# Modulation vectors computed with the conditioning vectors as 32-column weights, four chunks of the sum in four quarters of the TensorE array

## The reference, cut to what matters

```python
mod_ctx = (jax.nn.silu(c_ctx) @ w_mod[l] + b_mod[l])[None, None, :]
mod_lat = (jax.nn.silu(c) @ w_mod[l] + b_mod[l])[:, None, :]
...
sh1, sc1, g1, sh2, sc2, g2 = jnp.split(mod.astype(x.dtype), 6, axis=-1)
h = rmsnorm(x, norm1_g) * (1 + sc1) + sh1
m, st = mixer(h, w_in, ...)        # projections, RG-LRU scans, pooling, w_up_rnn, w_o
x = x + g1 * m
h = rmsnorm(x, norm2_g) * (1 + sc2) + sh2
x = x + g2 * peer(h, ...)          # 8 heads, top-16 product keys, expert rows
```

## Time and profile before

| | |
|---|---|
| median of 3 runs | 2282.52 us (2277.72 to 2285.01) |
| profiled execution, its own time | 2282.51 us |
| its span in the trace | 2280.2 us |
| PE busy | 2170.3 us, 95% of the span |
| DVE busy | 1673.6 us, 73% |
| ACT busy | 799.4 us, 35% |
| POOL busy | 775.4 us, 34% |
| mean granted TensorE clock | 0.964 of full |

### The profile page before, as it was taken

How to read it: one execution, slowest core, us unless ns; L and a number is a source line. 1 busy time by engine, 2 the same in 40 slices (tenths; PEclk the granted TensorE clock), 3 DMA queues, 4 the chain that set the end, 5 groups by cost and what they waited for, 6 DMA issues and landing times.

```text
span 2280.2 us, 34404 instructions
## 1 busy us (share of the span) xinstructions
PE 2170.3 (95%) x11688; PEld 1941.6 (85%) x11688; DVE 1673.6 (73%) x3317; ACT 799.4 (35%) x1028; POOL 775.4 (34%) x519
## 2 busy tenths in 40 slices
PE   5889998899999999999599999999999999999998
PEld 2789998899999888888488889998888888888887
DVE  4448998142449679999878888886777777777784
ACT  1435554211332322222144455554222222222222
POOL 1122331322123388888442222210222322322240
PEclk8999999899799999999799999999999999999997
DMA  8212213233422388888477777764999889989991
GB/s 354 84 52 65 66 61 115 98 121 130 163 78 66 114 265 283 292 290 285 151 281 290 292 269 289 283 254 161 309 320 310 305 312 363 310 308 310 318 325 66
DMA packets 167478, 502.06 MB, mean 220 GB/s; under 512 B 16608, under 2 KB 74336, under 8 KB 165600
## 3 DMA queue, kind: packets, MB, share of 16 engines
q1 hardware_dynamic: 101872, 273.96, 35.0%
q0 software_dynamic: 46080, 167.79, 21.4%
q10 hardware_dynamic: 19440, 59.25, 6.5%
HBM read 436.45 MB, written 64.50 MB: 220 GB/s over the span
## 4 chain that ended last, share of the span: by engine, by line
PE 75%; DVE 16%; DMA 2%; issue 2%; POOL 2%; ACT 2%; SPq 0%; ACTq 0%; DVEq 0%; POOLq 0%
PE P L787 29%; PE P L533 20%; PE P L702 14%; PE P L724 4%; PE P L551 3%; DVE rowsX L1430 2%; DVE rows L1430 2%; PE P L619 1%; POOL wLo L467 1%; DVE oh L1468 1%; DMA tb<-in_posT 1%; DVE oh L1461 1%; DVE keysel L1472 1%; PE P L755 1%; PE P L667 1%
## 5 line engine op out<-in xcount | busy, mean ns | idle before, releaser
L811 ACT ACTIVATE wHi<-raw 128x1024 fp32r<-128x1024 f32 x330 | 346.3, 1049 | 1257.3 <-PE P L787 459.2
L702 PE MATMUL P<-hHi,wHi 128*128 128x480 f32 x1024 | 397.1, 388 | 30.0 <-POOL wLo L467 29.8
L702 PE MATMUL P<-hHi,wLo 128*128 128x480 f32 x1024 | 390.6, 381 | 0.0
L702 PE MATMUL P<-hLo,wHi 128*128 128x480 f32 x1024 | 390.1, 381 | 0.0
L461 POOL TENSOR_TENSOR wLo<-raw,wHi 128x1024 fp32r<-128x1024 f32 (+1 forms) x76 | 186.6, 2457 | 511.3 <-ACT wHi L811 511.2
L1538 DVE TENSOR_TENSOR wLo<-raw,wHi 128x1024 fp32r<-128x1024 f32 x188 | 230.3, 1225 | 172.2 <-ACT wHi L811 171.3
L483 POOL DMA_INDIRECT rows<-in_v_tab,Eg x160 | 175.2, 1095 | 531.5 <-DVE htok L1589 248.8
L533 PE MATMUL P<-hHi,wHi 128*128 128x320 f32 x960 | 230.3, 321 | 23.4 <-POOL wLo L461 10.6
L702 PEld LDWEIGHTS P<-hHi,wHi 128*128 128x128 f32 x1024 | 193.9, 189 | 63.6 <-issue 33.0
L533 PE MATMUL P<-hLo,wHi 128*128 128x320 f32 x960 | 222.3, 313 | 0.0
L533 PE MATMUL P<-hHi,wLo 128*128 128x320 f32 x960 | 221.9, 312 | 0.0
(11 more groups left out here) (231 smaller groups left out, 3878.0 us busy)
## 6 DMA issues: line engine op xcount, KB each, us to landing
raw<-in_ublk SPq DMA_DIRECT2D x128, 512.0 KB, 4.5
raw<-in_v_tab SPq DMA_DIRECT2D x128, 512.0 KB, 5.7
raw<-in_wblk SPq DMA_DIRECT2D x104, 512.0 KB, 3.7
gel_scratch<-gel ACTq DMA_DIRECT2D x128, 240.0 KB, 4.2
gsr<-gel_scratch SPq DMA_DIRECT2D x128, 240.0 KB, 5.9
gate_scratch<-stage ACTq DMA_DIRECT2D x6, 4096.0 KB, 14.9
gates4a<-gate_scratch SPq DMA_DIRECT2D x16, 768.0 KB, 7.4
gates4b<-gate_scratch SPq DMA_DIRECT2D x16, 768.0 KB, 7.6
```

Source lines behind the costliest of these rows:

```text
L702: last = nc.tensor.matmul(P[0][:, j % 2, 0:TD], w_[:, j % 2, k * 128:(k + 1) * 128], x_[:, k, C0:T], start=(k == 0 and a == 0 and b == 0), ...
L811: return nc.scalar.activation(out, in_, f, **kw)
```

## The change

Modulations 16 to 39 are computed another way; 40 to 47 stay. DVE writes the conditioning vectors into `c32`, eight chunks of 32 columns, of which 2 hold the vectors and 30 are zero. `modulation_parts` (L568 of the changed file) takes a chunk of `c32` as weights and lets the 128 columns of the block's chunk pass through. Chunks 0 to 3 go to the four column quarters of the array and so to the partitions 0, 32, 64 and 96 on of `P[2]`; chunks 4 to 7 are added to them there. ACT copies the 128 x 128 result to `mrow` (`mod_rows`), and `modulation_turn` (L577) uses it as weights against two columns of `same`, which sums the four quarters and turns the result into the two columns of `P[3]` that were there before. A turn stands behind the next product, ahead of the next block's parts; the last one stands behind `norm_sum(1)`, since `P[2]` is used by both. DVE now waits for the turns (`mod_tr`).

```diff
+TURN = {m: n for n, m in enumerate(m for name, m in stream() if name == "mod" and 16 <= m < 40)}
...
+        def modulation_parts(m):
+
+            n, b = POS["mod", m], TURN[m]
+            pe.wait_ge(s["c32_ready"], 1)
+            pe.wait_ge(raw_ld[n % RAW], n // RAW * 16 + 16)
+            if b >= 2:
+                pe.wait_ge(s["mrow_ready"], b - 1)
+            for a in range(0, KC, 4):
+                for j in range(4):
+                    k = a + j
+                    last = nc.tensor.matmul(P[2][32 * j:32 * j + 32, b % 2, 0:128], c32[:, k, :],
+                                            raw[:, n % RAW, k * 128:(k + 1) * 128], start=(a == 0), stop=(a > 0),
+                                            tile_position=(0, 32 * j))
+            last.then_inc(raw_used[n % RAW], 1)
+
+        def modulation_turn(m):
+
+            pe.wait_ge(s["same_ready"], 1)
+            pe.wait_ge(s["mrow_ready"], TURN[m] + 1)
+            nc.tensor.matmul(P[3][:, MODB(m), MODC + m * 2:MODC + m * 2 + 2], mrow[:, TURN[m] % 2, :], same[:, 0:2],
+                             start=True, stop=True).then_inc(s["mod_tr"], 1)
...
+        unturned = []
+
+        def turn_parts():
+            while unturned:
+                modulation_turn(unturned.pop(0))
+
         def modulations(name, m):
+            turn_parts()
             for n in after(name, m):
-                modulation(n)
+                if n < 40:
+                    modulation_parts(n)
+                    unturned.append(n)
+                else:
+                    modulation(n)
...
+        pe.wait_ge(s["mrow_ready"], len(TURN))
         norm_sum(1)
+        turn_parts()
...
+        def mod_rows(name, m):
+            for n in after(name, m):
+                used(act, "mod", n)
+                if TURN[n] >= 2:
+                    act.wait_ge(s["mod_tr"], TURN[n] - 1)
+                actf(mrow[:, TURN[n] % 2, :], P[2][:, TURN[n] % 2, 0:128], ACT.Copy).then_inc(s["mrow_ready"], 1)
...
                 if n == 1:
                     split(G["wo", k] + 2)
+                    mod_rows("wo", k)
                     evicted(act, "wo", k)
...
             ga_out(m)
+            mod_rows("ga", m)
...
             split(G["upr", m] + 2)
+            mod_rows("upr", m)
             if m + 6 < KC:
                 ga_out(m + 6)
+                mod_rows("ga", m + 6)
...
-            if m0:
+            if m0 in (16, 30):
+                dve.wait_ge(s["mod_tr"], m0 + cnt - 16)
+            elif m0:
                 used(dve, "mod", m0 + cnt - 1)
...
+        ch.link(V.memset(c32[:, :, :], 0.0))
+        dve.wait_ge(s["c_ready"], 1)
+        ch.wait()
+        V.tensor_copy(c32[:, :, 0:2], cvec[:, :].rearrange("p (k g) -> p k g", g=2)).then_inc(s["c32_ready"], 1)
```

More of the change, by code:

```diff
@@ L192, in build @@
     csig = sb("csig", [128, KC * 2])
+    c32 = sb("c32", [128, KC, 32])
+    mrow = sb("mrow", [128, 2, 128])
     rinv = sb("rinv", [128, 6, 2])
@@ L302, in build @@
              "w_hi act_held eg_ready gel_free bank_free gmm_done oh_ready sm_ready tr2_done wf_ready "
-             "whi_ready wlo_ready same_ready sum_done hi_first rinv_ready rrow_done val_done ctx_ready crow_mm crow_ready crow_tr mod_read").split()
+             "whi_ready wlo_ready same_ready sum_done hi_first c32_ready mrow_ready mod_tr rinv_ready rrow_done val_done ctx_ready crow_mm crow_ready crow_tr mod_read").split()
     gel_st = [sem(f"gel_st{j}") for j in range(2)]
```

## The result

| | before | changed |
|---|---|---|
| median | 2280.12 us (4 runs, 2275.98 to 2285.01) | 2258.68 us (4 runs, 2256.43 to 2261.14) |
| ratio | | 0.9906, 95% interval 0.989 to 0.9922 |
| profiled execution, its own time | 2282.51 us | 2260.35 us |
| span | 2280.2 us | 2258.5 us |
| PE busy | 2170.3 us | 2143.1 us |

The change took 21.4 us off, 0.94%. The forecast was 2276 us with 2264 to 2290 as the range. So the direction was right, the size three times too small.

A forecast was written before the change was run, and what follows sets the result against it. TensorE was taken to bound the kernel, with 20 modulations on its path: 1.43 us in place of 1.79 each, 7.2 us gained, less 0.5 for the last turn, 6.7 off 2282.51, said as 2276 us; range 2264 to 2290.

The forecast's parts named there:

- What lies on the path: Between 360 and 660 us, 20 of the 24 modulations, 19 to 38, were said to be on the path.
- (a): Ahead of the high parts for `wo` 0, ACT's copy delays them 0.28 us; costed at nothing, 0.3 without cover.
- (b): Behind `wo` 1, copies queue behind the split of `wo` 2; no wait, or 0.55 us with `wo` 1 at full clock.
- all four quarters at once: Rival, chance 0.17: parts of 0.44 us, a modulation 0.88, net gain 17.2 us, time 2265 us.
- (c): In the second norm, ACT's last square comes some 0.5 us later behind the last copy; costed at nothing, 0.5 without cover.
- The price of the parts: Eight matmuls, 16 records per modulation, quarters partly overlapping: nine steps, 9 x 0.11 = 0.99 us.
- the full case: Lower bound for the parts with four records at a time: 4 x 0.11 = 0.44 us.
- The second reason: Issue of the parts' records: shortest distance 0.065 us, from L590, so 16 x 0.065 = 1.04 us.
- The switches: Switching the array to quarters and back once per modulation: 0.11 us, twice, 0.22 us; ends 0.12 and 0.33.
- The turn: One matmul of the old form per modulation, two records: 2 x 0.108 = 0.22 us.
- The last turn: Between the norm's sum and modulations 40 to 47: two records 0.42 us, with the switch 0.5 us added.
- the 1.5 kept to either side: Clock allowance: 1.5 us is the cost of one fall to 1.2 GHz in `wo` 1; 0 taken in the sum.

The follow-up runs named there:

- grouped variant: The changed kernel with the two matmuls of each quarter placed next to each other in program order; 2258.79 us, ratio 0.9891 to the kernel before.
- e7: The changed kernel with modulations 30 and 31 put back in the form of before; 2263.14 us, ratio 0.9892 to the kernel before.

## Why the prediction was wrong

**What lies on the path** was right: 20 modulations, 19 to 38; modulations 16 to 18 and 39 gave nothing; PE alone bounds the stretch. The three places where ACT's copies might come late cost 0.16 us or less. (a) The chain now passes through the copy ahead of the high parts (0.26 us at 499.97), and the stretch from the transfer for `wo` 1 to `wo` 0's rest grew by 0.16. (b) The 0.55 us of waiting feared for a `wo` 1 at full clock didn't come: the split of `wo` 2 began 4.5 us after modulation 31 and not 6.07, and both copies were done at 515.5 us, 1.4 us ahead of the turns. The rival "all four quarters at once" had 0.5 us for it. (c) From the end of `wo` 7 to the norm's sum it is 4.91 us where it was 4.82.

**The price of the parts** is the step that failed: "the second has to follow the first, but the first of the next matmul, on another quarter, can run beside it. That gives nine steps for 16 records, 9 x 0.11 = 0.99 us." It measured 0.57. The grouped variant shows that order does not bind at all, and the line through 16, 8 and 4 records that each quarter works for itself, 0.1075 us a record and 0.14 besides. The 0.44 of the full case was the right number for four lanes; two blocks in a row (1.01 us) differ from one (0.57) by just 0.44. The wrong term is thus 0.99 in place of 0.44: 0.55 us too much, 20 times, 11 of the 15 us between the forecast gain and the measured one.

**The second reason**, that issue would hold the pace at 0.065 us a record, was wrong as well. L590's spacing was at weights of 128 columns; 16 records with 32 weight columns took 0.57 us in all, 0.036 each, and 16 further short ones 0.12. I had taken a row with another weight width for a bound.

**The switches**, put at 0.22 us together, were right in size: 0.22 us is what a modulation pays once besides its parts and its turn, where the kernel before pays 0.01.
**The turn**, put at 0.22 us, was right too: a second one adds 0.22 us (0.34 - 0.12). That a single one shows only 0.12 comes from where the chain draws the line between neighbours.

By the measured period a modulation now costs 7.92 - 7.04 = 0.88 us, and 0.91 x 20 = 18.2 us, the very term of the rival, and it is put together as the rival had it: 0.44 for the parts, 0.22 for the turn and 0.22 for the changes. The last turn and its surroundings cost 0.64 us up to `wq` 0 (30.00 us from the norm's sum to `wq` 0 in place of 29.36), 0.5 expected. Product `wq` 0 behind it was 0.56 us shorter (8.93 for 9.49), so that nothing of this is left at its end. The clock gave 1.45 us in `wo` 1 and some 0.4 in modulations 30 and 31, a little more than the 1.5 kept to either side, and the old form at that place brings the loss back (8.68 us). Neither this nor the start of `ga` 5, 0.95 us earlier, was in the forecast; that both fell on the side of the gain is luck. With `ga` 5 itself (0.24), the shorter `wq` 0 and the 0.5 of (b) they make up the 4.1 us between the rival's 17.2 and the 21.3 of the chains, within 0.4. The chance of 0.17 for the full overlap was too low: no row of the trace spoke for order between quarters, I had only assumed it, and the range should have reached to that case's own lower end. Even that, 2265 less 1.5 for the clock, would have stood 5 us above the measured time.

## What to carry to other kernels

Matmuls with 128 weight columns and two columns passing took as long here as matmuls with 128 columns passing (1.68 us and 1.84 us for 16 records). So swap the operands, and if the new weights have 32 columns or fewer, put four chunks of the sum in the four quarters and add them in the matmul that turns the result. The swap alone loses: its period was 9.39 us against 8.83, since the turn comes on top. The quarters make the gain, and what counts is the number of records on the busiest one. Put several such blocks next to each other where that can be done: the 0.22 us for going there and back is paid once for all of them. Where a bound of such a thing is missing in a trace, give the full effect its chance and its place in the range before a mechanism that only one's reasoning supports. Before a variant is taken as the one without some cost, look at what its built program contains: the one that named no quarter used a quarter all the same. When work is moved, look at whose copies are queued behind it: moving one set of transposes by a product cost 4.3 us of waiting.

## What of the hardware was not expected

- Quarters have their own order: four records in a row for one quarter delay nothing for the others (0.59 us against 0.57), and records on different quarters start 0.007 us apart.
- Going from a product to the parts and back costs 0.22 us once, with one block or with two between; to matmuls of full width with two columns passing, 0.01 us.
- A turn with 32, 64 or 2 weight rows, between a product and the parts, costs 0.31 us on the path, with 128 rows, 96 of them zero, 0.12.
- Two modulations that let two columns pass, some 5 us behind an idle stretch of PE, were followed by half clock without a further idle moment, in both profiles that have them (0.50 from 524 to 526 us before, 0.53 and 0.62 in the 4 us behind them in e7). Two more of them 9 us later in the kernel before were not (1.00), nor was the same work with 128 columns passing.
